# Modulation of a two-block transformer kernel: from column matmuls to a fused multiply and sum on VectorE

## The chip, the cores and the metric

One Trainium2 chip, one of its cores. The metric is the device time of one execution in microseconds, the median of several. The profile is that of one further execution, and its own time stands beside its span below.

## The reference

The program computes two blocks on 512 tokens of width 1024. The first has attention in compressed, selected and window form, a recurrent branch (rg_lru), a cross attention and an MLP. The second has two layers, each with two gated FFNs and a mixer of a state-space part and a forgetting attention. Everything in the second block is modulated by a vector that depends on the input `c` alone:

```
for l in range(2):
    mod = (silu(c) @ mod_w[l] + mod_b[l]).reshape(bsz, 3, 3, 1024)     # mod_w[l] is 1024 x 9216
    pre(x, i)      = rms_norm(x, norm_pre[l, i]) * (1 + mod[:, i, 1]) + mod[:, i, 0]
    post_add(x, y) = x + res_w * mod[:, i, 2] * rms_norm(y, norm_post[l, i])
```

So `mod` is a vector times a matrix, twice: 2 x 9216 outputs, each a sum over 1024 inputs. The weights are 75.5 MB in fp32. Nothing of the first block needs the result; the first `pre` of the second block, at about 1292 us, does.

## The kernel before

The large products run on TensorE in high and low halves: a block of weights (128 x 2048 columns, 1 MB) lands in one of three slots `w`, ScalarE copies it into `wh` (line 1133, the high part), VectorE subtracts (`lo`, line 1772, into `wl`), and TensorE runs three matmuls for each pair of tiles (lines 578 to 580). A tile of 8 k-steps is 24 matmuls. Each engine has its own instruction stream, written out in the same order of stages by hand; they wait on each other's counted semaphores, which a first pass over the program records by name (`at(...)`).

The modulation is spread over the first block as small steps, called ticks. After each finished tile of a stage, and at set places in the attention loops, every engine that takes part calls `tick()`:

- SyncE (`mod()`, line 402) loads the tile of tick m, 128 inputs by 768 outputs (384 KB), into one of two slots `mslots`, once VectorE is done with tick m - 2. It stands in the same queue as the weight blocks, which `ahead(b)` issues two blocks in advance, each once its slot is free.
- VectorE (`tick`, line 1747) multiplies the tile by the scalar silu(c) of each partition and adds it to `macc`, 128 x 768 (line 1762 for the first of eight k-steps, line 1765 for the other seven).
- TensorE (`tick`, line 463) runs at every eighth tick a group: it waits for the accumulation, then multiplies six 128-column pieces of `macc` with a column of ones, which sums over the partitions (line 471). In the profile such a product is two matmul records, so a group has 12.
- VectorE adds the bias in the next such tick (line 1754) into `modc`, after it has waited for the group.

There are 192 ticks: 24 groups of 768 outputs by 8 k-steps. They lie, in order: 21 in the projections (stages v, g, k, c, q); 16 in the first attention pass (`NSA_ROWS`, one in four of 64 score blocks, each block with a maximum on VectorE, line 1923, and an exponential on ScalarE, line 1274); 48 in the second pass (`NSA_KEYS`, eight head pairs p of eight steps j, ticks at j = 1 to 6, with the next pair's `cmp_soft` at j = 2, which follows the scores that end with the mask matmul, line 731, and its scaling at j = 3; TensorE needs that at j = 6 in `cmp_turn`); 8 in stage r (convolution, gates and a scan per tile on VectorE, ScalarE and GpSimd); 2 each in mk and mv; 16 in the cross attention, interleaved with the tiles of stage m; the rest in m, o and the MLP. Each of the attention passes ends with a barrier of all engines.

At the cross attention, SyncE issues w_xo and the third block of stage m after the last matmul of mv, and the tiles of ticks 93 and on behind them. VectorE's stream is: four ticks in mk and mv, the split of the second m block, the gating of two m tiles, then the first maximum of the cross attention (line 2056). In front of the first stage, ScalarE computes squares (line 1161), casts XH (line 1186) and then casts the first weight block.

Of the kernel before, what the change touches and what calls it, by code (L numbers as in the profile page):

```python
# [28 lines left out]
def _cols(table, items):  # L29
    at = 0  # L30
    for name, n in items:
# [9 lines left out]
                 ("b_a", 8), ("b_i", 8), ("lam", 8), ("mod_b", 144), ("npre", 48), ("npost", 48), ("c", 8),  # L41
# [131 lines left out]
def program(nc, A, out, marks_in):  # L173
# [4 lines left out]
    with ctx:  # L178
# [40 lines left out]
        with nc.sbuf_tensor("lower", [128, 4096], F32), nc.sbuf_tensor("GH", [128, 4, 512], F32R) as GH, \  # L219
# [7 lines left out]
        const_landed, x_landed, w2_landed, rg_landed, mem_landed, xo_landed = [sem(n) for n in (  # L227
            "const_landed", "x_landed", "w2_landed", "rg_landed", "mem_landed", "xo_landed")]
# [86 lines left out]
        csil = cols[:, 0:8]  # L315
# [70 lines left out]
        def _(sp):  # L386
# [5 lines left out]
            sp.dma_start(w2s[1], A["cmp_v2"].rearrange("p (a b) -> p a b", a=2)).then_inc(w2_landed, 16)  # L392
            ticks = 0
# [7 lines left out]
            def mod():  # L401
                nonlocal ticks
                m = ticks
                ticks += 1
                if m >= 192:
# [42 lines left out]
        def _(pe):  # L448
            mm = nc.tensor.matmul
            pe.wait_ge(const_landed, 48)  # L450
            ticks = 0


            user = {2: None, 7: None}
            side = 2
# [133 lines left out]
            def run(s, xh, xl=None, xw=None, after=None):  # L589
                for whole in gemm(s, xh, xl, xw):  # L590
                    if whole:
                        if after is not None:
                            after()
                        tick()
# [2238 lines left out]
```

## Time and profile before

| | us |
|---|---|
| median of 3 runs (lowest, highest) | 3781.28 (3779.35, 3783.71) |
| the profiled execution | 3785.34 |
| its span, first to last instruction | 3783.4 |
| mean granted clock of TensorE | 0.949 of full |
| TensorE busy with matmuls | 3551.7 (94%) |
| VectorE, ScalarE, GpSimd busy | 1569.1, 1293.4, 471.5 |
| ticks on VectorE | 168 of line 1765, 24 of line 1762 |
| matmuls of line 471 | 288, in 24 groups of 12 |
| groups in the second attention pass start at | 366.8, 392.3, 424.5, 449.1, 474.6, 504.3 |
| first attention pass, second pass, stage r | about 200 to 346, 351 to 515, 515 to 602 |

Busy time is the sum over an engine's instructions. TensorE's matmuls are pipelined, and a busy TensorE can still be slower than at its peak. The line numbers are those of the kernel before. The granted clock is the share of full speed that TensorE was given.

### The profile page before, as it was taken

The page shows a single profiled execution, that of the slowest core. Times are in us where ns is not written, and L with a number is a line of the kernel's source. Part 1 is how long each engine was busy: PE and PEld are TensorE (multiplying, and loading weights), DVE is VectorE, ACT ScalarE, POOL GpSimd, SP SyncE. Part 2 cuts the span into 40 slices and gives each one's busy share as a digit, 9 for nine tenths or more (in the row PEclk, how much of TensorE's full clock was granted, in tenths as well). Part 3 has the DMA queues.
Part 4 walks back from the last instruction along what each step waited for, and adds up shares of the span by engine and source line. Part 5 has one row for each costly group of instructions (what it writes and reads, how often), then busy time and mean ns, then how long its engine had stood idle before and what let it go on. Part 6 is the DMA issues. An engine that isn't in the chain of part 4 may idle for free.

```text
span 3783.4 us, 39945 instructions
## 1 busy us (share of the span) xinstructions
PE 3551.7 (94%) x16654; PEld 2787.9 (74%) x16654; DVE 1569.1 (41%) x1962; ACT 1293.4 (34%) x1866; POOL 471.5 (12%) x367
## 2 busy tenths in 40 slices
PE   6988995999999999999999899999999899989997
PEld 5754454677888788877758788878887775878886
DVE  4655354444444363554423322245354542332233
ACT  3255354533222323232453322233322245332222
POOL 0100001051222010011102100011001120121001
PEclk9998997998999899998999899989999899989999
DMA  4332342343444133322312122223342230312221
GB/s 151 134 108 74 109 146 89 106 154 136 156 156 170 64 114 128 133 67 89 113 43 100 62 94 100 87 70 117 129 135 79 89 112 25 110 56 101 100 89 56
DMA packets 83684, 392.96 MB, mean 104 GB/s; under 512 B 9008, under 2 KB 17712, under 8 KB 50096
## 3 DMA queue, kind: packets, MB, share of 16 engines
q1 hardware_dynamic: 71376, 369.89, 28.6%
q10 hardware_dynamic: 12128, 20.52, 1.5%
q8 instruction: 132, 2.16, 0.2%
q14 instruction: 48, 0.39, 0.0%
HBM read 371.50 MB, written 18.87 MB: 103 GB/s over the span
## 4 chain that ended last, share of the span: by engine, by line
PE 77%; issue 12%; DVE 5%; ACT 3%; POOL 2%; DMA 1%; SPq 0%; DVEq 0%; ACTq 0%; POOLq 0%
PE pb L578 18%; PE pb L580 18%; PE pb L579 18%; PE pb L599 3%; PE pb L553 2%; PE pb L545 2%; PE pb L546 2%; PE pb L767 1%; PE pb L785 1%; PE pb L748 1%; PE pb L499 1%; POOL XL L2517 1%; PE pb L500 1%; PE pb L471 1%; PE pb L502 1%
## 5 line engine op out<-in xcount | busy, mean ns | idle before, releaser
L1772 DVE TENSOR_TENSOR wl<-w,wh 128x2048 fp32r<-128x2048 f32 (+3 forms) x270 | 596.5, 2210 | 1086.5 <-ACT wh L1133 1086.0
L578 PE MATMUL pb<-XH,wh 128*128 128x512 f32 (+1 forms) x2600 | 1029.0, 396 | 7.6 <-DVE wl L1772 6.8
L580 PE MATMUL pb<-XH,wl 128*128 128x512 f32 (+1 forms) x2600 | 1015.9, 391 | 0.0
L579 PE MATMUL pb<-XL,wh 128*128 128x512 f32 (+1 forms) x2600 | 1015.8, 391 | 0.0
L1133 ACT ACTIVATE wh<-w 128x2048 fp32r<-128x2048 f32 (+3 forms) x270 | 482.6, 1788 | 299.7 <-PE pb L580 201.8
L578 PEld LDWEIGHTS pb<-XH,wh 128*128 128x128 f32 (+1 forms) x2600 | 489.0, 188 | 113.6 <-DVE wl L1772 7.0
L579 PEld LDWEIGHTS pb<-XL,wh 128*128 128x128 f32 (+1 forms) x2600 | 489.0, 188 | 105.5 <-issue 3.4
L580 PEld LDWEIGHTS pb<-XH,wl 128*128 128x128 f32 (+1 forms) x2600 | 488.2, 188 | 105.9
L2575 POOL TENSOR_TENSOR HL<-tmps,HH 128x512 fp32r<-128x512 f32 x120 | 168.6, 1406 | 1398.7 <-ACT HH L1422 1398.7
L578 PE MATMUL pb<-HH,wh 128*128 128x512 f32 x720 | 285.8, 397 | 0.0
L580 PE MATMUL pb<-HH,wl 128*128 128x512 f32 x720 | 284.8, 396 | 0.0
L579 PE MATMUL pb<-HL,wh 128*128 128x512 f32 x720 | 284.7, 395 | 0.0
L1765 DVE SCALAR_TENSOR_TENSOR mreg<-mreg,cols 128x768 f32<-128x768 f32 x168 | 179.2, 1066 | 59.5 <-DMA mreg<-in_mod_w 56.7
L1422 ACT ACTIVATE HH<-tmps 128x512 fp32r<-128x512 f32 x120 | 75.6, 630 | 370.3 <-DVE tmps L2367 354.6
L599 PE MATMUL pb<-cf,tmps 128*128 128x1 f32 x704 | 132.2, 319 | 45.9 <-ACT tmps L1161 25.7
L599 PEld LDWEIGHTS pb<-cf,tmps 128*128 128x128 f32 x704 | 132.6, 289 | 52.0 <-ACT tmps L1473 16.9
L580 PEld LDWEIGHTS pb<-HH,wl 128*128 128x128 f32 x720 | 135.3, 188 | 32.7
L578 PEld LDWEIGHTS pb<-HH,wh 128*128 128x128 f32 x720 | 135.4, 188 | 32.1
L579 PEld LDWEIGHTS pb<-HL,wh 128*128 128x128 f32 x720 | 135.3, 188 | 32.2
L1548 ACT ACTIVATE tmps<-pb 128x512 f32<-128x512 f32 x88 | 52.8, 600 | 308.1 <-PE pb L580 289.6
L2367 DVE TENSOR_TENSOR tmps<-tmps,pb 128x512 f32<-128x512 f32 x88 | 60.4, 687 | 191.8 <-PE pb L580 191.8
L545 PE MATMUL pb<-HH,wh 128*128 128x512 f32 x240 | 96.0, 400 | 15.4 <-DVE tmps L2367 9.9
(411 smaller groups left out, 4132.8 us busy)
## 6 DMA issues: line engine op xcount, KB each, us to landing
w<-in_f_in SPq DMA_DIRECT2D x88, 1024.0 KB, 5.0
mreg<-in_mod_w SPq DMA_DIRECT2D x192, 384.0 KB, 3.1
w<-in_f_out SPq DMA_DIRECT2D x32, 1024.0 KB, 4.9
w<-in_w_up SPq DMA_DIRECT2D x16, 1024.0 KB, 5.4
w<-in_w_dn SPq DMA_DIRECT2D x16, 1024.0 KB, 5.3
w<-in_m_g SPq DMA_DIRECT2D x16, 1024.0 KB, 5.0
w<-in_w_m SPq DMA_DIRECT2D x12, 1024.0 KB, 5.3
w<-in_f_out SPq DMA_DIRECT2D x16, 768.0 KB, 4.2
```

What stands on the lines that cost most here:

```text
L545: mm(dst, hi[:, cs], xh[:, k, :], start=k == 0, stop=False)
L546: mm(dst, lo[:, cs], xh[:, k, :], start=False, stop=False)
L553: x = mm(dst, hi[:, cs], xl[:, k, :], start=False, stop=k == kts - 1)
L578: mm(dst, hi[:, cs], xh[:, k, :], start=k == 0, stop=False)
L579: mm(dst, hi[:, cs], xl[:, k, :], start=False, stop=False)
L580: x = mm(dst, lo[:, cs], xh[:, k, :], start=False, stop=fin)
L599: x = mm(bank[:, i:i + 1], squares[:, i * 128:(i + 1) * 128], c("mcol"), start=first and i == 0, stop=last and i == n // 128 - 1, skip_gro ...
L1133: actf(whl[i % 2][0][:, 0:s.cols], wslots[b % 3][:, 0:s.cols], ACT.Copy).then_inc(*AC.up(("hi", b)))
L1422: actf(HH[:, j, :], t[:, :], ACT.Copy).then_inc(*AC.up(("hh", *name, j)))
L1765: stt(out=macc[:, :], in0=mslots[t % 2][:, :], scalar=csil[:, k:k + 1], in1=macc[:, :], op0=ALU.mult, op1=ALU.add).then_inc(*DV.up(("mod_a ...
L1772: tt(low[:, 0:s.cols], wslots[b % 3][:, 0:s.cols], h[:, 0:s.cols].bitcast(F32), ALU.subtract).then_inc(*DV.up(("lo", b), ("w_free", b)))
L2575: tt(HL[:, j, :], t[:, :], HH[:, j, :].bitcast(F32), ALU.subtract).then_inc(*PO.up(("hl", *name, j)))
```

## The change

The weights are laid out by output: a tile is now 128 outputs (partitions) by 1024 inputs (columns), 512 KB, and there are 144. `silu(c)` is held as 1024 columns, the same in all 128 partitions. A tick is one instruction on VectorE: multiply the tile by `csil`, sum along the columns starting from the bias, write one column of `modc`. TensorE's ticks, the accumulator `macc`, the separate bias addition and the waits between TensorE and VectorE go. The 16 ticks of the first attention pass go too, and SyncE first issues all weight blocks of that pass and then the 48 tiles of the second. `c` is loaded by SyncE as a 128 x 1024 block (512 KB) after the other constants, and its Silu on ScalarE moves from the first instruction to right before stage v.

In the diff the first `tick()` is TensorE's, the second VectorE's.

```diff
-    NSA_ROWS += [("s", _n)] + [("j", 0)] * (_n % 2) + [("m", 0)] * (_n % 4 == 3) + [("c", 0)] * (_n == 57) + [("y", 0)] * (_n == 59)
+    NSA_ROWS += [("s", _n)] + [("j", 0)] * (_n % 2) + [("c", 0)] * (_n == 57) + [("y", 0)] * (_n == 59)
...
-        mreg = sb("mreg", [128, 2304])
-        mslots = [mreg[:, 768 * i:768 * i + 768] for i in range(2)]
-        macc = mreg[:, 1536:2304]
+        mreg = sb("mreg", [128, 3072])
+        mslots = [mreg[:, 1024 * i:1024 * i + 1024] for i in range(2)]
+        csil = mreg[:, 2048:3072]
...
             sp.dma_start(w2s[1], A["cmp_v2"].rearrange("p (a b) -> p a b", a=2)).then_inc(w2_landed, 16)
+            sp.dma_start(csil, A["c_rows"]).then_inc(c_landed, 16)
...
                 if m >= 2:
-                    sp.wait_ge(*at("mod_acc", m - 2))
-                sp.dma_start(mslots[m % 2][:, :], A["mod_w"][m // 32, m // 8 % 4, m % 8]).then_inc(mod_landed[m % 2], 16)
+                    sp.wait_ge(*at("mod", m - 2))
+                sp.dma_start(mslots[m % 2], A["mod_w"][m]).then_inc(mod_landed[m % 2], 16)
...
                 if s.name == "qx":
-                    for n in range(64):
-                        ahead(s.b[0] + min(n // 3, 4))
+                    ahead(s.b[0] + 4)
+                    for n in range(48):
                         mod()
...
-            def tick():
-                nonlocal ticks
-                t, ticks = ticks, ticks + 1
-                if t % 8 == 0 and 0 < t <= 192:
-                    gi = t // 8 - 1
-                    pe.wait_ge(*at("mod_acc", t - 1))
-                    take(side, ("modc", gi))
-                    for j in range(6):
-                        x = mm(banks[side][:, j:j + 1], macc[:, j * 128:(j + 1) * 128], c("one"), start=True, stop=True)
-                    x.then_inc(*TE.up(("mod_mm", gi)))
...
-            actf(csil, p("c", 0, 8), ACT.Silu).then_inc(*AC.up(("silu",)))
             actf(u1, p("lam", 0, 8), ACT.Abs).then_inc(*AC.up())
...
+            act.wait_ge(c_landed, 16)
+            actf(csil, csil, ACT.Silu).then_inc(*AC.up(("silu",)))
             run(st_of["v"], copy_to(lambda j: V[:, j, :]))
...
-                if t % 8 == 0 and 0 < t <= 192:
-                    gi = t // 8 - 1
-                    idx, half = gi // 4, gi % 4
-                    dve.wait_ge(*at("mod_mm", gi))
-                    tt(modc[idx][:, half * 6:half * 6 + 6], banks[side][:, 0:6], p("mod_b", idx * 24 + half * 6, 6),
-                       ALU.add).then_inc(*DV.up(("modc", gi)))
-                if t < 192:
-                    k = t % 8
+                if t < 144:
                     dve.wait_ge(mod_landed[t % 2], 16 * (t // 2 + 1))
                     if t == 0:
                         dve.wait_ge(*at("silu"))
-                    if k == 0:
-                        ts(macc[:, :], mslots[t % 2][:, :], csil[:, 0:1], None, ALU.mult).then_inc(*DV.up(("mod_acc", t)))
-                    else:
-                        dve.wait_ge(*at("mod_acc", t - 1))
-                        stt(out=macc[:, :], in0=mslots[t % 2][:, :], scalar=csil[:, k:k + 1], in1=macc[:, :],
-                            op0=ALU.mult, op1=ALU.add).then_inc(*DV.up(("mod_acc", t)))
+                    v.tensor_tensor_reduce(out=mslots[t % 2], in0=mslots[t % 2], in1=csil, scale=1.0, scalar=p("mod_b", t),
+                                           op0=ALU.mult, op1=ALU.add, accum_out=modc[t // 24][:, t % 24:t % 24 + 1]).then_inc(
+                        *DV.up(("mod", t)))
```

## Rows read from the trace of the kernel before

**Rows 1.** The chain of work that ended last, shares by engine
```profile
PE 77%; issue 12%; DVE 5%; ACT 3%; POOL 2%; DMA 1%; SPq 0%; DVEq 0%; ACTq 0%; POOLq 0%
```

**Rows 2.** Instructions by tile (ns min/median/max) and by shape (busy us, mean ns)
```profile
L1765 DVE SCALAR_TENSOR_TENSOR mreg<-mreg,cols x168: 1004/1012/2019, 47.4 to 1214.7; 128x768 f32<-128x768 f32 x168
...
L2105 DVE SCALAR_TENSOR_TENSOR XL<-tmps,modc,XH x48: 739/744/747, 1310.3 to 3402.1; 128x512 fp32r<-128x512 f32 x48
...
L1818 DVE TENSOR_TENSOR XL<-tmps,XH 128x512 fp32r<-128x512 f32 x16 | 10.1, 683 | 0.0
L2005 DVE TENSOR_TENSOR_SCAN tmps<-tmps 128x512 f32<-128x512 f32 x8 | 9.8, 1224 | 0.3
```

**Rows 3.** Line 471: idle time of TensorE before it, what ended it, times
```profile
  DVE mreg L1765: 44.9, 12
```

**Rows 4.** Timeline of a dense stage around a group: start us, us, what
```profile
947.80 0.39 PE L580 MATMUL pb<-XH,wl 128*128 128x512 f32 x1
948.03 1.39 PE L471 MATMUL pb<-cf,mreg 128*128 128x1 f32 x12
...
949.28 0.49 PE L578 MATMUL pb<-XH,wh 128*128 128x512 f32 x1
```

**Rows 5.** Timeline of TensorE, second attention pass: the mask matmul
```profile
362.00 0.27 PE L731 MATMUL pb<-cb 128*128 128x256 bf16 x1
...
405.87 0.27 PE L731 MATMUL pb<-cb 128*128 128x256 bf16 x1
...
422.97 0.27 PE L731 MATMUL pb<-cb 128*128 128x256 bf16 x1
...
488.19 0.27 PE L731 MATMUL pb<-cb 128*128 128x256 bf16 x1
```

**Rows 6.** Windows: length, busy by engine, PEclk, DMA share, GB/s
```profile
383.00:406.00 23.00, 22.17 (x130) 11.04 (x129) 7.91 (x15) 7.13 (x11) 0.00 (x0) 0.85 0.35 104
406.00:423.00 17.00, 17.00 (x113) 7.91 (x111) 8.25 (x14) 7.13 (x11) 0.00 (x0) 1.00 0.50 140
...
488.00:515.00 27.00, 26.62 (x183) 12.64 (x181) 12.84 (x20) 10.66 (x17) 0.00 (x0) 1.00 0.45 132
```

**Rows 7.** Timeline behind stage mv: SyncE's issue, VectorE's ticks, TensorE's group, first maximum
```profile
637.60 0.39 SPq L420 DMA_DIRECT2D BIG<-in_w_xo  x1
...
649.00 2.14 DVE L1765 SCALAR_TENSOR_TENSOR mreg<-mreg,cols 128x768 f32<-128x768 f32 x2 [25.10 <-DMA mreg<-in_mod_w]
...
654.17 2.72 PE L471 MATMUL pb<-cf,mreg 128*128 128x1 f32 x12 [16.60 <-DVE mreg L1765]
...
670.65 0.42 DVE L2056 TENSOR_REDUCE st<-pb 128x1 f32<-128x256 f32 x1
```

**Rows 8.** The chain in order of time: ticks and the group of stage r
```profile
175.84 1.00 DVE mreg L1765
...
345.45 0.94 DVE mreg L1765
...
551.96 2.52 PE pb L471 x12
```

**Rows 9.** DMA issues by line: size of each, median us to landing
```profile
mreg<-in_mod_w SPq DMA_DIRECT2D x192, 384.0 KB, 3.1
...
w<-in_glu SPq DMA_DIRECT2D x16, 512.0 KB, 3.7
```

**Rows 10.** Timeline, last pair of the second attention pass, VectorE and ScalarE
```profile
488.50 0.42 DVE L1894 TENSOR_REDUCE cols<-pb 128x8 f32<-128x256 f32 x1 [9.79 <-PE pb L731]
...
508.66 1.02 ACT L1302 ACTIVATE tmps<-pb 128x1024 f32<-128x1024 f32 x1 [1.70 <-PE pb L773]
...
514.66 0.60 ACT L1310 ACTIVATE BIG<-pb 128x512 f32<-128x512 f32 x1 [0.54 <-PE pb L785]
```

**Rows 11.** Timeline of ScalarE at the start: a table load, the first weight cast
```profile
11.74 1.28 ACT L1123 ACT_TABLE_LOAD   x1 [11.74 <-DMA hT<-in_x]
...
40.32 3.69 ACT L1133 ACTIVATE wh<-w 128x2048 fp32r<-128x2048 f32 x2
```

More of the change, by code:

```diff
@@ L40 @@
 NPR = _cols(PR, [("g_mix", 8), ("g_mlp", 8), ("g_final", 8), ("g_mem", 8), ("conv_w", 32), ("conv_b", 8),
-                 ("b_a", 8), ("b_i", 8), ("lam", 8), ("mod_b", 144), ("npre", 48), ("npost", 48), ("c", 8),
+                 ("b_a", 8), ("b_i", 8), ("lam", 8), ("mod_b", 144), ("npre", 48), ("npost", 48),
                  ("fb", 16), ("are", 64), ("aim", 64), ("ldt", 64), ("pos_k", 16), ("pos_v", 16)])
@@ L226, in program @@
         mod_landed = [sem(f"mod_landed{i}") for i in range(2)]
-        const_landed, x_landed, w2_landed, rg_landed, mem_landed, xo_landed = [sem(n) for n in (
-            "const_landed", "x_landed", "w2_landed", "rg_landed", "mem_landed", "xo_landed")]
+        const_landed, x_landed, w2_landed, rg_landed, mem_landed, xo_landed, c_landed = [sem(n) for n in (
+            "const_landed", "x_landed", "w2_landed", "rg_landed", "mem_landed", "xo_landed", "c_landed")]
         zero_stored, drive_stored, lag_stored = [sem(n) for n in ("zero_stored", "drive_stored", "lag_stored")]
@@ L404, in mod @@
                 ticks += 1
-                if m >= 192:
+                if m >= 144:
                     return
                 if m >= 2:
-                    sp.wait_ge(*at("mod_acc", m - 2))
-                sp.dma_start(mslots[m % 2][:, :], A["mod_w"][m // 32, m // 8 % 4, m % 8]).then_inc(mod_landed[m % 2], 16)
+                    sp.wait_ge(*at("mod", m - 2))
+                sp.dma_start(mslots[m % 2], A["mod_w"][m]).then_inc(mod_landed[m % 2], 16)
             blocks = [(s, g) for s in stages for g in range(len(s.srcs))]
@@ L450, in _ @@
             pe.wait_ge(const_landed, 48)
-            ticks = 0
             user = {2: None, 7: None}
-            side = 2
             def take(b, label):
@@ L593, in run @@
                             after()
-                        tick()
             def token_sums(bank, squares, n, first, last):
@@ L652, in attend @@
                         turn(n - 1, units[n - 1])
-                    tick()
                     next(job, None)
@@ L794, in _ @@
                     next(job, None)
-                elif what == "m":
-                    tick()
                 elif what == "c":
@@ L812, in _ @@
                 if what == "t":
-                    side = home(n // 8 + 1)
                     nsa_keys(n)
@@ L820, in _ @@
                     cmp_turn(n)
-                elif what == "m":
-                    tick()
-            side = 2
             barrier(TE, pe, "nsa")
@@ L865, in _ @@
                 x.then_inc(*TE.up(("xo", j)))
-            for whole in job:
-                if whole:
-                    tick()
+            for _ in job:
+                pass
             def sums_after(r):
@@ L891, in _ @@
             spread("final", 512)
-            while ticks <= 192:
-                tick()
             def y_sums(r):
@@ L1984, in _ @@
             for what, n in NSA_KEYS:
-                if what == "t":
-                    side = home(n // 8 + 1)
-                elif what == "c":
+                if what == "c":
                     cmp_soft(n)
@@ L2090, in _ @@
                     op1=ALU.mult).then_inc(*DV.up(("h_new", "final", k)))
-            while ticks <= 192:
+            while ticks < 144:
                 tick()
@@ L2783, in _layout @@
     d["w_dn"] = np.stack([_blocks(f("w_down")[0][1024 * q:1024 * q + 1024], 256) for q in range(4)])
-    mw = f("mod_w_2").reshape(2, 8, 128, 3, 4, 768).transpose(0, 3, 4, 1, 2, 5)
-    d["mod_w"] = np.ascontiguousarray(mw).reshape(6, 4, 8, 128, 768)
+    d["mod_w"] = np.ascontiguousarray(f("mod_w_2").transpose(0, 2, 1)).reshape(144, 128, 1024)
+    d["c_rows"] = np.broadcast_to(f("c_2").reshape(1, 1024), (128, 1024))
     gu = [t for i in range(11) for t in (2 * i, 2 * i + 1, 22 + 2 * i, 23 + 2 * i)]
```

4 lines of the change are left out of this document (removed).

## The prediction

> **What bounds the kernel now.** The first view to read is the chain of work that ended last: TensorE holds 77% of the span, VectorE 5%, DMA 1% [rows 1]. An edit is therefore worth what it takes out of TensorE's queue, plus the waits of TensorE that end with it. Work on VectorE counts only where TensorE waits for it.
>
> Next comes what the modulation costs. VectorE runs 192 ticks, 168 of them fused with a median of 1.01 us [rows 2]. TensorE runs 24 groups of 12 matmuls (line 471), and stood idle for 44.9 us, over both of its queues, until line 1765 ended [rows 3]. One group in the large matmul stages shows the undisturbed price: it starts at 948.03 and the next matmul starts at 949.28, so 1.25 us; a large matmul before it has a pitch of 0.23 [rows 4].
>
> In the second attention pass a group costs far more. The cmp_scores mask matmul (line 731) comes once per head pair. Between 405.87 and 422.97 no group ran, and the period was 17.10 us. From 362.00 to 488.19 there are six periods, and the table above has five groups in them: 126.19 - 6 x 17.10 = 23.6 us of excess, 4.7 us per group, nearly four times the plain price [rows 5]. The windows show why: the granted clock was 0.85 of full in a stretch with a group and 1.00 in the one without [rows 6]. A group is a wait, then twelve one-column matmuls, and the clock drops behind it.
>
> Last, the longest wait. After the mv stage TensorE is idle for 16.6 us, until 654.17, and then runs a group [rows 7]. The reader should see that this is not arithmetic. SyncE passes the end of the last mv matmul at 637.60, queues w_xo and two blocks of w_m first, and only then the tiles of ticks 93 and 94. VectorE waited 25.1 us for them, until 649.00, and TensorE's group waits for tick 95.
>
> **The change, part by part.**
>
> *The groups in plain stages.* Groups 0 to 3 and 14 to 23, 14 in all, lie in dense stages: 14 x 1.25 = 17.5 us off [rows 4].
>
> *The second attention pass.* Five groups take 23.6 us with them; the sixth, late in the last pair, cost about 1.4. Together 25 us off. This supposes that the clock stays at full, as in the period without a group [rows 5, 6].
>
> *The rest on TensorE.* Group 10, in the r stage, is on the chain with 2.5 us [rows 8]: 2.5 off. Groups 12 and 13, in cross attention, are 2.5 together, taken below with the ticks.
>
> *The stall after mv.* It shrinks but does not vanish. VectorE still ticks four times in mk and mv, and SyncE still issues those tiles behind the same 3 MB. What goes is TensorE's own wait: it now runs the two ready tiles of m (48 matmuls at 0.227, 10.9 us) while VectorE waits. VectorE gets its first tile at about 649.4 (3.4 MB came in the 11.4 us to 649.0, and 0.13 MB more takes 0.4), ends ticks at 650.7 and 652.0, waits 3.7 for each next tile [rows 9], ends the fourth tick near 657, splits the m weights by 659.5, gates two tiles and gives the first maximum near 662. Now that first maximum is at 670.65 [rows 7]. So 9 off. TensorE is now idle from 648.5 to 659.5 and likely starts at the half clock again, for which I take back 0.5. Net 8.5 off.
>
> *The first attention pass.* It loses its 16 ticks. None is on the chain there except the last one, at 345.45, in front of nsa_pads: 0.9 off [rows 8].
>
> *The new tick.* No row shows a multiply with a running sum. Nearest are the fused op of two SBUF operands, 1.012 us at 768 columns and 0.744 at 512 [rows 2], which is 1.047 ns per column: 1024 columns give 1.28 us. The subtraction (0.683 at 512) would give 1.22. The other end is the scan, 1.224 us at 512 [rows 2], which also carries a state from column to column: twice the slope, 2.3 us at 1024. I take 1.28, since the sum feeds back through one addition alone, where the scan feeds back through two operations. VectorE's total stays much as it is (144 x 1.28 = 184 us; 168 x 1.01 = 170 and the 24 shorter ticks now), but each tick is 0.27 longer where TensorE waits for one. Those places are the end of the q stage (on the chain [rows 8], 0.3 on), the r stage (four of eight ticks, 1.1 on) and cross attention. There VectorE's loop is maximum, scale, tick; but TensorE is nearly full too, so of 16 x 0.27 = 4.3 about 2.5 shows, and groups 12 and 13 give 2.5 back: zero.
>
> The Trainium skill, "Vector Engine (DVE) Microarchitecture Reference", section "Points that are easy to get wrong", says that the scalar_tensor_tensor form with two non-bf16 SBUF sources runs at half rate because no port is left for reading the accumulator back. The trace disagrees for the plain form: its 1.047 ns per column is one column per cycle of 0.96 GHz. No row here shows the form with an accumulator. By that rule the tick would be about 2.3 us and the sum below about -5 instead of -49.
>
> *Cadence in the second attention pass.* VectorE must do six ticks in 17.1 us from two slots. A slot turns in landing plus tick. For landing I take 3.7 us, the row of another 512 KB load; 384 KB takes 3.1 [rows 9]. That is 3.7 + 1.28 = 5.0. From one maximum of cmp_soft to the next come two ticks and 2.9 us of softmax and waits (5.5), then two turns of the slower slot, 15.5 us in all: under 17.1. The tail is tighter. After the last cmp_soft at 488.50 [rows 10] eleven ticks remain: the first ends 2.3 later, five more turns of its slot make 27.3, so 515.8. The pass without its group would end near 515.3 - 1.4 = 513.9. So VectorE holds the barrier for about 1.9: 2 on.
>
> *The start.* The small Silu (0.2) goes from ahead of the first squares, and a 1024-column Silu with a table load goes between the last XH cast and the first weight cast (40.32), on which TensorE's first product hangs through the split. A load takes 1.28 [rows 11] and a 1024-column activation 1.02 [rows 10]: 2.3 on, 0.2 off, so 2.1 on. Whether the table load at 11.74 stays for the Abs that now comes first is not in the trace; if not, 1.3 less.
>
> The Trainium skill, "ScalarE: Activation LUTs", section "Table sets: the hidden batching unit", lists abs among cheap functions that every set has. By it one of the two early loads could vanish and the start would cost 0.8 instead of 2.1; no run shows it yet.
>
> *At no cost.* The extra 512 KB (c_rows) lands long before 40 while ScalarE and TensorE do the first norm; uncovered it would be 3.7. Per tile of a dense stage 1024 KB moves instead of 896, in 5.4 us, and the weights are two blocks ahead. In the first attention pass SyncE now loads all weight blocks before it issues a tile; no tick waits there.
>
> **The sum.** -17.5 - 25 - 2.5 - 8.5 - 0.9 + 0.3 + 1.1 + 0 + 2 + 2.1 = -48.9 us. The profiled execution took 3785.3 us (span 3783.4, 2 outside it), so the changed one should take 3736. The median of the runs is 3781.3, 4 lower; taken from that, 3732.
>
> **The rivals.**
>
> *Half-rate sum* (slow tick, 2.3 us). For it: the scan row. Against it: reductions and fused ops at one column per cycle. Prices against my tick: cross attention 16 more, r stage about 6, the mv stall 3, q's end 1; the second pass needs 19.5 us per pair where TensorE needs 17.1 (about 10, after the slack in front of cmp_turn) and ends 7 later. Together 43: the gain falls to about 6, so 3775. Chance 0.10.
>
> *VectorE becomes the bound, slower.* The same mechanism past its turning point: above 1.8 us per tick each further us costs about 24 in the pairs, 6 at the pass's end, 16 in cross attention, 8 in r and 3 at the stall, 57 in all. From 3775 it takes 0.25 us more to be 0.2% slower; a tick of 2.6 us or more decides it. At 2.8 us: 3775 + 0.5 x 57, about 3803. Nothing in the trace speaks for such a tick. Chance 0.05.
>
> *The clock drops stay, or the stall does.* TensorE also waits briefly for ScalarE in each step of the second pass; if such gaps lower the clock without the groups, only the plain price returns: 6 x 1.25 = 7.5 instead of 25. Or the mv stall keeps its length because VectorE's part is what ends it. Against it: from 488 to 515 the clock was 1.00, these waits and the last group in it [rows 6]. The gain would be 20 to 35, so about 3753. Chance 0.13.
>
> **How the numbers follow.** My forecast, a gain of 38 to 60 (3721 to 3743), has 0.72. Within it the tick varies from 1.22 to 1.5, the start from 0.8 to 2.3, the stall from 6 to 10. The range for 8 in 10 reaches into the third rival: 3718 to 3757. A difference of 0.2%, 7.6 us, is about what can be told from no change. Half rate sits at its edge, so: faster 0.86, within it 0.08, slower 0.06.
>
> **What the profile after would show.** Line 471 is gone and TensorE has some 288 matmuls fewer. The new tick's mean stands between 1.2 and 1.4 us; 2.3 would be the rival. The mask matmul of the second pass comes every 17.1 us at a clock near 1.00. Behind mv, two m tiles run at once, then a wait of about 11 us for VectorE. The first product starts about 2 us later than now. VectorE's last tick of the second pass ends after ScalarE's last activation. The last tick starts well before 1100 (now at 1214.7 [rows 2]). The prediction is wrong if the tick is above 1.8 us, or if periods of 21 us stay.

## The result, and the profile after

The changed kernel takes 3738.95 us (median of 4 runs, 3733.43 to 3744.03), the one before 3780.32 in the same comparison (3778.48 to 3783.71): a ratio of 0.9889 [0.987, 0.9908], 41 us less. The forecast was 3732 in a range of 3718 to 3757. Timed once more, the same kernel took 3732.33 against 3777.67, 0.9883 [0.987, 0.9897]. Its profiled execution was the slowest of its four (3744.03, span 3741.9). The four lie 11 us apart, and their granted clock goes with it, 0.951 to 0.956 of full, lowest for the longest. The four of the kernel before lie 5 apart here, but seven of them in another comparison 11 (3774.26 to 3785.40), so the spread isn't the changed kernel's own.

The page of the changed kernel: busy time by engine; the chain that ended last; the new tick; its transfers.

```profile
PE 3510.3 (94%) x16366; PEld 2751.8 (74%) x16366; DVE 1568.6 (42%) x2034; ACT 1293.8 (35%) x1866; POOL 475.5 (13%) x367
...
PE 77%; issue 12%; DVE 5%; ACT 3%; POOL 2%; DMA 1%; SPq 0%; DVEq 0%; POOLq 0%; ACTq 0%
...
L1730 DVE CUSTOM_DVE_ANT_0 mreg<-mreg,pr 128x1024 f32<-128x1024 f32 x144 | 190.5, 1329 | 72.3 <-DMA mreg<-in_mod_w 72.0
...
mreg<-in_mod_w SPq DMA_DIRECT2D x144, 512.0 KB, 3.6
```

The chain has the same shares as before [rows 1]: an average over the span does not see an edit that takes from TensorE's queue and TensorE's waits alike. Line 471's 288 matmuls are gone.

The tick's row by tile (duration min/median/max in ns, first and last start in us):

```profile
L1730 DVE CUSTOM_DVE_ANT_0 mreg<-mreg,pr x144: 1270/1279/2383, 48.1 to 996.4; 128x1024 f32<-128x1024 f32 x144
```

The median is 1.279 us for 1024 columns, just what the fused op of rows 2 gives at that width: the forecast had 1.28 from it, and 2.3 as its other end. So the running sum adds nothing that this comparison can tell. The last tick starts at 996.4, before at 1214.7 [rows 2].

**The second attention pass.** The mask matmul of cmp_scores (now line 715), one per head pair, in TensorE's timeline:

```profile
362.30 0.27 PE L715 MATMUL pb<-cb 128*128 128x256 bf16 x1
...
379.41 0.27 PE L715 MATMUL pb<-cb 128*128 128x256 bf16 x1
...
464.97 0.27 PE L715 MATMUL pb<-cb 128*128 128x256 bf16 x1
```

and the windows of three stretches (length, busy PE, PEld, DVE, ACT, POOL, PEclk, DMA share, GB/s):

```profile
358.00:375.00 17.00, 17.00 (x112) 7.92 (x111) 8.61 (x18) 7.03 (x12) 0.00 (x0) 1.00 0.39 122
...
409.00:426.00 17.00, 17.00 (x112) 7.81 (x112) 9.37 (x19) 7.10 (x11) 0.00 (x0) 1.00 0.59 175
...
489.00:500.00 11.00, 5.69 (x23) 4.14 (x22) 3.02 (x8) 5.28 (x9) 0.00 (x0) 0.69 0.52 187
```

From 362.30 to 464.97 there are six equal periods, (464.97 - 362.30) / 6 = 17.11 us. Before, only the one period without a group was that long [rows 5]. TensorE is full and the clock stays at 1.00 (the 2.4 GHz level), where the stretch with a group had 0.85 [rows 6]. The last window shows a new idle time.

**The pass's end.** The timeline of ScalarE's last activation, VectorE's last ticks and TensorE's next matmul (in brackets: idle time before, and what ended it):

```profile
488.07 1.29 DVE L1730 CUSTOM_DVE_ANT_0 mreg<-mreg,pr 128x1024 f32<-128x1024 f32 x1 [1.56 <-DMA mreg<-in_mod_w]
...
490.05 0.60 ACT L1286 ACTIVATE BIG<-pb 128x512 f32<-128x512 f32 x1 [0.54 <-PE pb L769]
490.92 1.28 DVE L1730 CUSTOM_DVE_ANT_0 mreg<-mreg,pr 128x1024 f32<-128x1024 f32 x1 [1.56 <-DMA mreg<-in_mod_w]
...
493.81 1.28 DVE L1730 CUSTOM_DVE_ANT_0 mreg<-mreg,pr 128x1024 f32<-128x1024 f32 x1 [1.60 <-DMA mreg<-in_mod_w]
...
495.31 0.77 PE L564 MATMUL pb<-XH,wh 128*128 128x512 f32 x1 [5.31 <-issue]
```

ScalarE, which set the end before [rows 10], is done at 490.65. VectorE's last tick ends at 493.81 + 1.28 = 495.09, 4.4 us later, and only then does the next stage start. The 5.31 us stand under "issue", but the end of the tick names the cause. Ticks 488.07 and 493.81 use the same slot, so one turn of a slot takes 5.7 us, not 5.0.

**The stall behind mv.** TensorE's, then VectorE's timeline:

```profile
627.82 0.70 PE L611 MATMUL pb<-BIG,cf 64*128 64x256 f32 x2
639.88 0.79 PE L564 MATMUL pb<-XH,wh 128*128 128x512 f32 x1 [11.36 <-DVE wl L1738]
```

```profile
629.35 1.28 DVE L1730 CUSTOM_DVE_ANT_0 mreg<-mreg,pr 128x1024 f32<-128x1024 f32 x1 [25.89 <-DMA mreg<-in_mod_w]
...
637.53 2.29 DVE L1738 TENSOR_TENSOR wl<-w,wh 128x2048 fp32r<-128x2048 f32 x1
...
641.76 0.42 DVE L2019 TENSOR_REDUCE st<-pb 128x1 f32<-128x256 f32 x1
```

TensorE no longer waits in front of a group; it runs the two ready tiles of m, then stands for 11.36 us until VectorE has split the next weights. VectorE still waits for tiles behind the 3 MB, 25.89 us against 25.10 [rows 7]. SyncE queues w_xo at 617.00, 20.6 us earlier than before, and the first maximum comes 28.9 earlier, at 641.76.

**The start.** ScalarE:

```profile
12.22 1.28 ACT L1098 ACT_TABLE_LOAD   x1 [12.22 <-DMA hT<-in_x]
...
39.53 1.28 ACT L1175 ACT_TABLE_LOAD   x1
40.82 1.06 ACT L1175 ACTIVATE mreg<-mreg 128x1024 f32<-128x1024 f32 x1
41.79 3.69 ACT L1107 ACTIVATE wh<-w 128x2048 fp32r<-128x2048 f32 x2
```

The first weight cast is 1.5 us later than in rows 11. Before, a second load (13.36, for the Exp) followed the one of rows 11 (for the Silu); now one load, at 12.22, serves both Abs and Exp. One load of 1.28 us has gone. The Trainium skill, "ScalarE: Activation LUTs", section "Table sets: the hidden batching unit", lists abs among the functions that every set has; the trace agrees with it. The input x landed 0.5 us later in this execution.

**Where the 41 us come from.** The two programs run the same 16,366 matmuls outside line 471, in the same order. So I take the start of the same matmul in both traces: the table shows after minus before, us, cumulated, beside the forecast's own terms. The last column is a second profiled execution of the same changed kernel.

| before's time, us | what ends there | forecast | after | again |
|---|---|---|---|---|
| 60 | start | +2.1 | +2.2 | +1.5 |
| 351 | q stage, first attention pass (groups 0 to 3) | -3.5 | +0.6 | -4.2 |
| 488 | second pass, pairs | -27.1 | -23.2 | -28.2 |
| 518 | its end | -26.5 | -18.3 | -23.5 |
| 612 | r stage | -27.9 | -20.4 | -25.7 |
| 672 | stall behind mv | -36.4 | -28.2 | -34.4 |
| 732 | cross attention | -36.4 | -25.9 | -33.8 |
| 1240 | dense stages | -48.9 | -40.9 | -51.4 |
| 3700 | rest of the kernel | -48.9 | -41.3 | -53.2 |

Two things are to be seen. Nearly all of the gain lies before 1240, where the ticks end. And two executions of one program differ by 4.8 us at 351 and by 12 at the end. Of the 4.8, 1.5 appear around 243 and 1.5 between 244 and 304, where the first execution's granted clock fell and the second's did not. Windows of the first:

```profile
242.00:248.00 6.00, 5.42 (x22) 3.15 (x22) 1.67 (x6) 2.85 (x11) 0.00 (x0) 0.72 0.27 115
293.00:299.00 6.00, 5.63 (x22) 2.91 (x22) 1.63 (x6) 2.70 (x12) 0.00 (x0) 0.72 0.00 0
```

and of the second:

```profile
242.00:248.00 6.00, 6.00 (x31) 3.38 (x29) 2.85 (x6) 4.30 (x13) 0.00 (x0) 1.00 0.00 0
293.00:299.00 6.00, 6.00 (x36) 3.52 (x33) 3.31 (x8) 3.71 (x14) 0.00 (x0) 1.00 0.00 0
```

So in what follows a single difference of a few us between two kernels' ends counts for nothing by itself; the same stretch read in several traces does.

### The profile page after: what moved, and what is told of

Read it like the earlier page. It is cut to its first block, busy times and chain, and to the rows that moved or that the text cites. A ratio compares the mean times of both kernels' runs of the same rounds, so it can differ in the third digit from the quotient of the medians.

```text
span 3741.9 us, 39203 instructions
## 1 busy us (share of the span) xinstructions
PE 3510.3 (94%) x16366; PEld 2751.8 (74%) x16366; DVE 1568.6 (42%) x2034; ACT 1293.8 (35%) x1866; POOL 475.5 (13%) x367
## 4 chain that ended last, share of the span: by engine, by line
PE 77%; issue 12%; DVE 5%; ACT 3%; POOL 2%; DMA 1%; SPq 0%; DVEq 0%; POOLq 0%; ACTq 0%
PE pb L564 18%; PE pb L566 18%; PE pb L565 18%; PE pb L584 3%; PE pb L539 2%; PE pb L531 2%; PE pb L532 2%; PE pb L751 1%; PE pb L769 1%; PE pb L732 1%; PE pb L485 1%; DVE wl L1738 1%; POOL XL L2480 1%; PE pb L486 1%; PE pb L488 1%
## 5 line engine op out<-in xcount | busy, mean ns | idle before, releaser
L1730 DVE CUSTOM_DVE_ANT_0 mreg<-mreg,pr 128x1024 f32<-128x1024 f32 x144 | 190.5, 1329 | 72.3 <-DMA mreg<-in_mod_w 72.0
```

What stands on the lines that cost most here:

```text
L1730: v.tensor_tensor_reduce(out=mslots[t % 2], in0=mslots[t % 2], in1=csil, scale=1.0, scalar=p("mod_b", t), op0=ALU.mult, op1=ALU.add, accum ...
```

## The experiments

Each ratio is against the kernel before, run on the same chip in the same comparison: 3782.83 us for the groups alone, the groups without wait, the shorter end and the tiles in time; 3776.21 for the wide groups, the early Silu, the doubled tick and all together; 3777.67 for the ticks of cross attention and those of the r stage.

**The groups alone.** The kernel before without TensorE's groups (it leaves out the partition sums of the modulation; VectorE's ticks and tiles stay, at their places and sizes; its wait for the group becomes one for its own accumulation):

```diff
-                if t % 8 == 0 and 0 < t <= 192:
-                    gi = t // 8 - 1
-                    pe.wait_ge(*at("mod_acc", t - 1))
-                    take(side, ("modc", gi))
-                    for j in range(6):
-                        x = mm(banks[side][:, j:j + 1], macc[:, j * 128:(j + 1) * 128], c("one"), start=True, stop=True)
-                    x.then_inc(*TE.up(("mod_mm", gi)))
...
-                    dve.wait_ge(*at("mod_mm", gi))
-                    tt(modc[idx][:, half * 6:half * 6 + 6], banks[side][:, 0:6], p("mod_b", idx * 24 + half * 6, 6),
+                    dve.wait_ge(*at("mod_acc", t - 1))
+                    tt(modc[idx][:, half * 6:half * 6 + 6], macc[:, 0:6], p("mod_b", idx * 24 + half * 6, 6),
```

In this kernel and the next two, VectorE also waits for its own previous instruction in front of the first of eight k-steps.

> The kernel before, with TensorE's groups taken out and VectorE adding the bias to the first columns of its accumulator instead: the sums over the partitions are left out, the 192 ticks, their tiles and their order stay. Theory (a group costs its matmuls, its wait and the clock behind it): 25 us in the second attention pass, 24 in the 18 others, about 9 at the stall behind mv, so 56 to 60 us faster than before, near 3722, and the mask matmul of the second pass every 17.1 us. Rival (a group costs only its 1.25 us of matmuls, the clock drops and the stall have other causes): 24 x 1.25 = 30 us, near 3750, and periods near 20 us stay.

Measured: 3729.91 us (3728.35 to 3730.99), 0.9861 [0.9845, 0.9878], 53 us under the kernel before. So the groups alone are worth as much as the whole change or more (41 and 45 us in its two comparisons; the intervals of the ratios overlap); the change also adds waits elsewhere. On the same matmuls it gains against the kernel before (times are those of before, here and below) 1.1 us up to 351, 24.4 in the second pass (351 to 488), 9.2 at the stall (612 to 672) and 17.9 from 732 to 1240. Its end of the pass gives nothing back (-25.5 at 488, -27.0 at 518). The same matmuls also tell each group's part at its place. The first two, at 98 and 147, return 1.2 and 1.4 us, the third nothing, the fourth 1.0, and each of the ten in the dense stages behind cross attention 1.3 to 1.4. These numbers are the same in this kernel and in both executions of the changed one.

**Is it the group's wait that lowers the clock?** The kernel before, with groups that don't wait for the accumulator (it leaves the modulation sums out: the matmuls read the identity):

```diff
-                    pe.wait_ge(*at("mod_acc", t - 1))
                     take(side, ("modc", gi))
                     for j in range(6):
-                        x = mm(banks[side][:, j:j + 1], macc[:, j * 128:(j + 1) * 128], c("one"), start=True, stop=True)
+                        x = mm(banks[side][:, j:j + 1], c("ident"), c("one"), start=True, stop=True)
```

> The kernel before, with the groups kept but fed by a constant matrix, so that TensorE no longer waits for the accumulation: the modulation sums are left out, the 288 one-column matmuls stay. If the clock drops of the second pass come from the wait in front of a group, its periods fall to 17.1 + 1.3 = 18.4 us, 15 us in five groups, and with about 10 at the stall the run is some 25 to 28 us faster, near 3754, with no half clock in the pass. If the one-column matmuls bring the clock down, only the waits go: 5 x 1.2 + 10, about 16 us, near 3765, and the granted clock of a period with a group stays near 0.85.

Measured: 3766.55 us (3758.73 to 3768.59), 0.9956 [0.9938, 0.9973]. Of the 24 us of the second pass it returns 8.2 (+2.1 at 351, -6.1 at 488). The wait for the accumulator is worth the stall (-10.5 from 518 to 672) and some of the gaps; the clock still drops behind the later groups. One caution: the group still waits for its bank (1.18 us in front of the one at 419.84), so not every gap was gone. The recorded alternative, that one-column matmuls bring the clock down, had a time near 3765, which is close, and a clock that stays near 0.85, which didn't come (0.95 and 0.90 below).

**Is it the thin matmuls, then?** The same, with groups of 128 columns where they had one (same waits, same count, sums left out as above):

```diff
-                        x = mm(banks[side][:, j:j + 1], c("ident"), c("one"), start=True, stop=True)
+                        x = mm(banks[side][:, 0:128], c("ident"), c("ident"), start=True, stop=True)
```

> The kernel before with groups that have no wait for the accumulation and stream 128 columns in place of one (identity times identity; the modulation sums are left out), otherwise as in the experiment with groups without a wait. If the thin products bring the clock down behind a group, the clock stays at 1.00 through the second attention pass here and the three half-clock stretches at 422, 446 and 470 us go, some 8 us faster than that experiment even though a group streams more. If the wait for the bank in front of a group does it, the stretches stay and the run is 0 to 3 us slower than it.

Measured: 3756.68 us (3755.27 to 3760.88), 0.9948 [0.9934, 0.9963]; the intervals of the two overlap, so the whole time doesn't tell them apart. The stretch does. Windows of the thin groups without wait:

```profile
351.00:412.00 61.00, 57.97 (x369) 28.91 (x369) 25.38 (x52) 24.04 (x37) 0.00 (x0) 0.95 0.37 106
412.00:482.00 70.00, 68.14 (x409) 33.40 (x408) 25.68 (x47) 24.18 (x37) 0.00 (x0) 0.90 0.39 117
```

and of the wide ones:

```profile
351.00:412.00 61.00, 59.88 (x379) 29.60 (x379) 24.80 (x47) 24.43 (x37) 0.00 (x0) 0.96 0.38 111
412.00:482.00 70.00, 68.14 (x448) 33.55 (x446) 30.42 (x57) 25.99 (x41) 0.00 (x0) 1.00 0.42 123
```

Between 412 and 482 both have TensorE busy for the same 68.14 us, so the gaps are alike in sum. They are alike in front of the groups too. The thin groups in TensorE's timeline:

```profile
419.84 1.50 PE L470 MATMUL pb<-cf 128*128 128x1 f32 x12 [1.18 <-DVE tmps L1900]
...
443.06 1.50 PE L470 MATMUL pb<-cf 128*128 128x1 f32 x12
...
468.48 1.85 PE L470 MATMUL pb<-cf 128*128 128x1 f32 x12 [0.68 <-ACT tmps L1260]
```

and the wide ones:

```profile
418.67 1.60 PE L470 MATMUL pb<-cf 128*128 128x128 f32 x12 [1.18 <-DVE tmps L1900]
...
440.47 1.60 PE L470 MATMUL pb<-cf 128*128 128x128 f32 x12
...
464.41 1.60 PE L470 MATMUL pb<-cf 128*128 128x128 f32 x12 [0.68 <-ACT tmps L1260]
```

The wait for the bank is the same 1.18 and 0.68 us, so by itself it doesn't bring the clock down here; and the group at 443.06 has no idle time in front, yet the clock over 443 to 450 is 0.76, with TensorE busy for all of the 7 us (440 to 447 with the wide group: 1.00, also 7 us busy). With thin groups the granted clock is 0.90 and 409 matmuls go through, with wide ones 1.00 and 448. On the same matmuls the thin ones gain 1.5 us on the kernel before from 421 to 481, the wide ones 6.8. What differs is the group's own matmuls: 251 ns (median) with one column, 275 with 128, 24 ns more, and the drop is gone. In the kernel before, this stretch had 0.91, and the one from 351 to 412 had 0.87. There the thin groups without a wait have 0.95 too. So in these traces, one execution of each kernel, both play a part: without the wait the early drops are gone, the later ones go with the thin matmuls. A kernel with the wait and wide matmuls was not run. And the thin matmuls don't do it everywhere: in the kernel before, the clock is 1.00 over 90 to 175 with two groups in it, and over 910 to 1240 with seven.

**The pass's end, with fewer ticks in it:**

```diff
-    NSA_KEYS += [("m", 0)] * (1 <= _j <= 6)
+    NSA_KEYS += [("m", 0)] * (1 <= _j <= (3 if _p == 7 else 6))
...
-                    for n in range(48):
+                    for n in range(45):
```

> The changed kernel, with the last three ticks of the second attention pass moved behind it (45 instead of 48 in the pass, all 144 still done, later). Theory (VectorE's ticks end 5 us behind TensorE's last product there, and the barrier and the half clock behind it are paid): TensorE's gap at the barrier falls from 5.2 us to under 1 and the run is 4 to 7 us faster than the changed kernel, 3732 to 3735. Rival (the barrier waits for something else, or stage r takes the time back since it is paced by VectorE and GpSimd): within 2 us of 3739.

Measured: 3733.17 us (3728.51 to 3739.05), 0.9872 [0.9855, 0.9889]. TensorE's timeline:

```profile
489.03 0.47 PE L564 MATMUL pb<-XH,wh 128*128 128x512 f32 x1 [0.74 <-ACT BIG L1286]
```

The next stage now waits 0.74 us, and for ScalarE's last activation instead of VectorE's tick. From 488 to 518 the execution gains 1.4 on the kernel before, where the changed kernel gives back 4.9 (again: 4.7). So in this execution the ticks at the end cost some 6 us there (1.4 + 4.9 = 6.3), shown by removing three of them; the forecast had 2.

Two things limit that number. First, some 2 us of it come back in stage r. From 518 to 612 the changed kernel gains 2.1 and 2.2 us (its two executions), this one nothing (0.0), so at 612 the net price is about 4. By the whole time the ratio is 6 us lower (0.9872 against 0.9889), within the intervals. Second, the price isn't the same in all traces. The four other traces with the same ticks at this place give back 4.7, 4.5, 4.3 and, in the next experiment's, 2.1 us from 488 to 518.

**The stall, with its tiles in time.** SyncE issues tiles in mk and mv too, ahead of w_xo:

```diff
-                    for n in range(4 + 16):
-                        ahead(s.b[0] + 1 + max(n - 4, 0) // 6)
+                    for n in range(16):
+                        ahead(s.b[0] + 1 + n // 6)
                         mod()
-                elif s.name not in ("cmp", "gr", "mk", "mv") and not (s.name == "m" and g < 3):
+                elif s.name not in ("cmp", "gr") and not (s.name == "m" and g < 3):
```

> The changed kernel, with SyncE issuing the four tiles of the ticks in mk and mv in those stages, ahead of w_xo and of the last block of m that wait for mv's end. Theory (TensorE's idle time of 12.5 us behind the first two m tiles, and the half clock after it, come from these tiles alone): the gap closes and the run is 13 to 17 us faster than the changed kernel, near 3724. Rival (the next thing is just as late: the weights of m behind w_xo, or VectorE's own work): at most 5 us faster, and another wait of 8 us or more stands in the same place.

Measured: 3725.89 us (3718.65 to 3727.36), 0.9848 [0.9832, 0.9864]. VectorE's timeline:

```profile
611.73 1.28 DVE L1730 CUSTOM_DVE_ANT_0 mreg<-mreg,pr 128x1024 f32<-128x1024 f32 x1 [10.31 <-DMA mreg<-in_mod_w]
...
624.64 0.41 DVE L2019 TENSOR_REDUCE st<-pb 128x1 f32<-128x256 f32 x1
```

The wait falls from 25.89 to 10.31 and the first maximum comes 17.1 us earlier than in the changed kernel. From 600 to 655 TensorE is busy for 51.65 us at a clock of 1.00, in the changed kernel for 42.98 at 0.80. On the same matmuls this kernel gains 21.1 us on the kernel before between 612 and 672, the changed one 7.8 and 8.7: 12 to 13 more. This confirms the forecast's reading that the order of SyncE's transfers made VectorE's wait. TensorE's group had added the 8 to 9 us that went with it.

**The Silu out of the start's chain.** In the changed kernel, the same two lines moved:

```diff
             squares("mix", lambda k: hT[:, k, :], 512)
+            act.wait_ge(c_landed, 16)
+            actf(csil, csil, ACT.Silu).then_inc(*AC.up(("silu",)))
...
-            act.wait_ge(c_landed, 16)
-            actf(csil, csil, ACT.Silu).then_inc(*AC.up(("silu",)))
             run(st_of["v"], copy_to(lambda j: V[:, j, :]))
```

> The changed kernel, with the Silu of the 1024 columns moved between ScalarE's squares and its root, where ScalarE waits 5 us for TensorE's sums. Theory (the Silu and its table load, 2.3 us in front of the first weight cast, set the first product): the first product starts 2.3 us earlier than in the changed kernel, at 43.8 in place of 46.1, and the run is 2 to 2.5 us faster. Rival (the cast or its split waits for something else, the weights' landing or the norm): no difference at the first product.

ScalarE's timeline:

```profile
22.18 1.28 ACT L1164 ACT_TABLE_LOAD   x1
23.48 1.06 ACT L1164 ACTIVATE mreg<-mreg 128x1024 f32<-128x1024 f32 x1
24.55 1.28 ACT L1139 ACT_TABLE_LOAD   x1
```

Load and Silu now run in ScalarE's 4.9 us of waiting, and the first product starts at 43.61, 2.45 earlier than the 46.06 of the changed kernel: the forecast's 2.3 on is confirmed at its place. At the end nothing of it can be told: 3739.19 us (3728.92 to 3740.72), 0.9893 [0.9874, 0.9911], against 0.9889. Two microseconds are less than the 12 by which two executions differ.

**The price of a slower tick.** Each tick done twice, one after the other (the values are others for it):

```diff
-                    v.tensor_tensor_reduce(out=mslots[t % 2], in0=mslots[t % 2], in1=csil, scale=1.0, scalar=p("mod_b", t),
-                                           op0=ALU.mult, op1=ALU.add, accum_out=modc[t // 24][:, t % 24:t % 24 + 1]).then_inc(
-                        *DV.up(("mod", t)))
+                    for rep in range(2):
+                        x = v.tensor_tensor_reduce(out=mslots[t % 2], in0=mslots[t % 2], in1=csil, scale=1.0,
+                                                   scalar=p("mod_b", t), op0=ALU.mult, op1=ALU.add,
+                                                   accum_out=modc[t // 24][:, t % 24:t % 24 + 1])
+                        if rep == 0:
+                            x.then_inc(*DV.up())
+                            own()
+                        else:
+                            x.then_inc(*DV.up(("mod", t)))
```

> The changed kernel, with each tick done twice (the second pass runs over the products of the first, so the modulation's values are other ones): VectorE is held 2.6 us per tick in place of 1.28, as a half-rate instruction would hold it. By the prediction's prices: 16 to 20 us in cross attention, 6 to 10 in stage r, about 10 in the pairs of the second pass and 7 at its end, 3 at the stall and 1 in q, so 45 to 60 us slower than the changed kernel, back at the time of the kernel before or above it (3784 to 3799). Rival (VectorE's idle half covers it): 10 to 20 us slower, near 3755.

Measured: 3798.89 us (3793.63 to 3802.91), 1.0058 [1.0043, 1.0073]: slower than the kernel before. That is 60 us over the changed kernel (3738.95, timed in another comparison; by the two ratios it is 64) for 1.28 us more per tick. So it is 47 to 50 us per us, where the rivals had 42 below their turning point (43 for 1.02) and 57 above it. By place, against the changed kernel on the same matmuls: 7 up to 178, 12 in the second pass's pairs, 9 at its end, 6 in the r stage, 2 at the stall, 11 in cross attention, 6 in the dense stages. So the projections do wait for ticks (I had 1), and cross attention less than the 16 put down for a tick 1.02 us longer. The forecast's rival, VectorE as the bound, lacked only the slow tick.

**No ticks in cross attention.** In the changed kernel `attend` calls no tick, and SyncE issues 4 tiles in place of 20 there; the 16 are done in later stages:

```diff
                         ahead(s.b[0] + 1 + max(n - 4, 0) // 6)
-                        mod()
+                        if n < 4:
+                            mod()
...
                     scale(n)
-                    tick()
                     next(job, None)
```

> The changed kernel without the 16 ticks of cross attention (done later, in m, o and the MLP). Theory (VectorE's loop of maximum, scale and tick is about level with TensorE there): 1 to 3 us faster than the changed kernel. Rival (the tick is wholly on the path, 16 x 1.28): 10 us or more faster.

Measured: 3735.97 us (3734.31 to 3736.95), 0.9887 [0.9873, 0.99], with 3732.33 for the changed kernel in the same comparison. From 672 to 732 it loses 1.9 us against the kernel before (-35.3 to -33.4), the unchanged one 0.5 and 2.3 in its two executions. No gain: as they stand the ticks there cost nothing that these runs can tell. Only the doubled tick shows a price.

**All of it together:** fewer ticks at the pass's end, tiles in mk and mv, the early Silu, no ticks in cross attention.

> The changed kernel with the three repairs together (three ticks of the second pass later, the four tiles issued in mk and mv, the Silu early) and without the 16 ticks of cross attention, which are done later in m, o and the MLP. If the repairs add up: 6 + 13 + 2 + 1.5, about 22 us faster than the changed kernel, near 3716. If they share one slack (a barrier that catches up what another gave): 14 to 16 us, near 3724.

Measured: 3718.63 us (3712.39 to 3725.21), 0.9846 [0.9831, 0.9861]. The interval overlaps that of the tiles in mk and mv alone (0.9848), so these runs don't show that the rest adds anything to the stall. Against the changed kernel it is 16 us by the two ratios (0.9846, 0.9889) and 20 by the medians, so whether the parts add up (22) or share one slack (14 to 16) isn't decided.

**The last ticks on the chain.** The same, without the 8 ticks of the r stage (they move behind it):

```diff
-                elif s.name not in ("cmp", "gr") and not (s.name == "m" and g < 3):
+                elif s.name not in ("cmp", "gr", "r") and not (s.name == "m" and g < 3):
...
-            run(st_of["r"], r_out)
+            for _ in evict(st_of["r"], r_out):
+                pass
```

> The kernel with the three repairs and no ticks in cross attention, now without the eight ticks of stage r as well, which is paced by the convolution and the scan on VectorE. Theory (four to eight of these ticks are on the path): 5 to 9 us faster than with them, near 3711. Rival (the stage is paced by ScalarE's and GpSimd's part of each tile): under 2 us.

Measured: 3700.13 us (3697.64 to 3706.84), 0.9794 [0.9781, 0.9808]. The windows of the r stage, with its ticks (the kernel of all edits together):

```profile
485.00:585.00 100.00, 69.67 (x243) 48.46 (x241) 70.24 (x76) 76.04 (x91) 22.29 (x16) 0.84 0.33 120
```

and without:

```profile
485.00:585.00 100.00, 74.04 (x269) 53.34 (x269) 61.41 (x70) 78.11 (x94) 24.24 (x16) 0.85 0.22 84
```

VectorE is busy 8.8 us less there and 26 more matmuls go through. Between 500 and 612, on the same matmuls, this kernel gains 10.7 us on the kernel before and the one with the ticks 1.3, so 9.4 more: eight ticks of 1.28 are 10.2. The tiles' transfers left the stage with them (84 GB/s for 120), and the doubled tick put the same eight at only 6, so how much of the 9.4 is VectorE's time alone isn't shown. The median is 18.5 us lower than that of all edits together, which was run in another comparison, where 5 to 9 had been expected. The 9 us beyond the stage are not accounted for; between the two profiled executions 4.8 lie behind 1240, where neither has a tick. This is the fastest version measured, 32 us under the changed kernel of its comparison and 2.1% under the kernel before.

## Why the prediction was right

The forecast named the sign, the size and the mechanism, with one term mis-sized (the pass's end) and one right by luck (the r stage). Point by point, by the table's two executions:

- *The second attention pass*, the largest term, -23.6 for five groups: measured -23.8 and -24.0 (351 to 488), and -23.8 to -24.1 in six traces more with the same pairs. The supposition that the clock stays at full without groups held: six equal periods at 1.00. The experiments add why: the waits in front of the groups and their one-column matmuls, each with a part of its own.
- *The stall*, -8.5: measured -7.8 and -8.7. The steps came as written down: two m tiles at once, a wait of 11.4 (forecast 11) for VectorE, and a lower clock behind it, 0.80 over 600 to 655 (0.91 in the second execution).
- *The plain groups*, -1.25 each: in the ten of the dense stages, 1.3 to 1.4 at each one's place, 13.6 together where 12.5 was forecast. The stages gave 15.0 and 17.6 in all; what is beyond 13.6 lies outside the groups. The four early ones did not all lie in dense stages, as the forecast had it: the third and fourth, at 239.3 and 306.5, lie in the first attention pass. The first two returned 1.2 and 1.4, the third nothing, the fourth 1.0: 3.6 for 5.0. The last tick of that pass returned 0.8 and 0.9, as forecast. That the sum up to 351 was +0.6 in one execution and -4.2 in the other is mostly the clock, as the windows at 242 and 293 show.
- *The new tick*, 1.28: measured 1.279. The half-rate rival (chance 0.10) and the one past it (0.05) fall. The running sum is read out once, by an instruction of 0.08 us at the end of each tick. The Trainium skill, "Vector Engine (DVE) Microarchitecture Reference", section "Points that are easy to get wrong", gives half rate to a scalar_tensor_tensor with two non-bf16 SBUF sources. The new tick is another instruction, to which the forecast carried that rule over (about 2.3 us, an estimate); the trace disagrees for it. From the doubled tick, 60 to 64 us for 1.28, a tick of 2.3 would have cost about 48 to 51 us in proportion, an estimate.
- *The end of the second pass*, +2 and -1.4: measured +4.9 and +4.7 for both, so the ticks' part is +6.1 to +6.3 where 2 was forecast. This is the term that was mis-sized. The mechanism (eleven ticks left, VectorE holds the barrier) was right; the step "A slot turns in landing plus tick" took 3.7 us for a landing. In this stretch the last five tiles took 4.3 to 4.5 from issue to landing, and the last turn 5.74. Five turns made 27.5 us where the forecast had 25, and the barrier came 4.4 us after ScalarE's end instead of 1.9. The rest is the clock: it is 1.00 over 490 to 492, 0.56 over 492 to 495 and 0.50 over 495 to 499, so it fell while TensorE stood still. The kernel with its tiles in time has the same ticks and the same two slots here, and its last four tiles landed in 3.5 to 4.2 us (median 3.7): there the last tick ended 2.1 us after ScalarE, as forecast. So the landing time sets the term, and it differs between executions; two tiles were on the way in both, so that alone isn't the reason, and the reason stays open.
- *The start*, +2.1: measured +1.5 at the first product (46.06 - 44.60). Silu and load cost 2.3 there as forecast; one other load went (-1.3), and x landed 0.5 later.
- *The r stage*, -1.4: -2.1 and -2.2 (518 to 612). Here the number agrees, but in these traces by luck. Where the stage starts in time, in the kernels with the shorter end, it gains nothing on the kernel before (0.0 and +0.2), and the groups alone return only 0.4 there. So the 2.5 for group 10 did not come back, and the 2 us measured are most likely the stage's catching up after the late barrier. *Cross attention*, 0: +2.3 and +0.5.

The forecast of 3732 lies 7 us under the first measurement and on the second. As a gain it was 48.9 us; measured were 41 and 45, and the second agreement in time is in part luck, since the kernel before, too, was 3.6 us faster in that comparison than the 3781.3 from which the forecast started. In the first profiled execution the difference of 7.6 us (-41.3 for -48.9) is +4.1 up to 351, +4.3 at the pass's end, +2.3 in cross attention, and -3.1 in the rest. In the second (-53.2) it is -0.7, +4.1, +0.5 and -8.2. Of these the pass's end alone is there in both executions with the same sign and near the same size; the surplus of the dense stages, 2.5 and 5.1, hides it in part.

What stays open: why the landings at the pass's end took longer in some executions; which share of a clock drop belongs to the wait and which to the thin matmuls, since the wait was never run with wide ones; and why the groups lower the clock in the attention pass and not in the dense stages.

## What to carry to other kernels

Price small work that is queued between large matmuls by what stands behind it, not by its own length: here 12 tiny matmuls cost 1.25 us by themselves, and 4.7 where a wait and a lower clock came with them. A series of transfer-bound steps at the end of a loop becomes the barrier once the loop gets faster, so count its turns with a range for the landing time: 3.7 or 4.4 us made a barrier that was 2 or 4.4 us late. And ask of each helper step, stage by stage, whether the engine it runs on is on the chain there: the eight ticks of the r stage, with their transfers, were worth some 9 us, the sixteen of cross attention nothing that could be told.

## What was unexpected of the hardware

- In the second attention pass groups of one-column matmuls went with a lower granted clock of TensorE even in a full queue: 0.90 of full over 412 to 482 with them, 1.00 with groups of 128 columns in their place, at the same 68.14 us of busy time and the same waits in front (one profiled execution of each). Each wide matmul took only 24 ns more (275 for 251). In the dense stages the same thin groups left the clock at 1.00 (90 to 175, 910 to 1240).
- A multiply of two 1024-column fp32 operands in SBUF with a running sum takes 1.279 us, with an instruction of 0.08 at its end for reading the sum: just what the plain fused op's two sizes in rows 2 give at that width (1.28).
- 512 KB landed in 3.6 us as a median, but in 4.3 to 4.5 for the last five tiles of the second pass; with the same ticks at the same place, another kernel's last four took 3.5 to 4.2.
